# Half the gather buffers, early gate weights in the freed megabyte, and one down matrix asked for sooner

## What is computed

```python
for e in range(N_EXPERTS):                       # 32 experts, 3 matrices of 1 MB each
    act = jax.nn.silu(hf @ w_gate[e]) * (hf @ w_up[e])
    y = y + combine[:, e:e + 1] * (act @ w_down[e])
```

## Time and profile before

| what | value |
|---|---|
| median of 3 executions | 1311.11 us |
| the profiled execution, its own time | 1308.09 us |
| its span on the core | 1306.3 us |
| PE busy | 1217.3 us, 93% of the span |
| DVE busy | 558.0 us, 43% |
| ACT busy | 307.9 us, 24% |
| POOL busy | 245.1 us, 19% |
| moved by DMA | 213.06 MB, mean 163 GB/s |
| granted TensorE clock, mean | 0.978 |

### The profile page before, as it was taken

How to read it: one execution, slowest core, us unless ns; L and a number is a source line. 1 busy time by engine, 2 the same in 40 slices (tenths; PEclk the granted TensorE clock), 3 DMA queues, 4 the chain that set the end, 5 groups by cost and what they waited for, 6 DMA issues and landing times.

```text
span 1306.3 us, 13442 instructions
## 1 busy us (share of the span) xinstructions
PE 1217.3 (93%) x5000; PEld 686.0 (53%) x5000; DVE 558.0 (43%) x1424; ACT 307.9 (24%) x725; POOL 245.1 (19%) x214
## 2 busy tenths in 40 slices
PE   6999989999989999999999899999999879977884
PEld 3555434455544444588884446776664544433342
DVE  2214493566547751208972367422232623222221
ACT  4313643433310000224022245300011311111110
POOL 6000023354500000071600030312300021211100
PEclk9999999999989999999999999999999979998898
DMA  9625112224265612313131102202257589999994
GB/s 330 115 73 129 65 70 60 104 76 144 86 207 191 225 57 89 113 65 129 65 119 74 57 9 65 70 1 65 65 191 323 213 314 385 407 403 406 416 404 143
DMA packets 92248, 213.06 MB, mean 163 GB/s; under 512 B 20186, under 2 KB 51306, under 8 KB 79848
## 3 DMA queue, kind: packets, MB, share of 16 engines
q1 hardware_dynamic: 78800, 191.56, 39.8%
q0 software_dynamic: 10176, 17.96, 5.7%
q10 hardware_dynamic: 3200, 2.61, 0.6%
HBM read 205.73 MB, written 14.75 MB: 169 GB/s over the span
## 4 chain that ended last, share of the span: by engine, by line
PE 76%; DVE 7%; SPq 6%; DMA 5%; ACT 3%; issue 2%; ACTq 0%; POOL 0%; POOLq 0%; DVEq 0%
PE PS L2280 7%; PE PS L995 6%; PE PS L638 5%; SPq L2766 5%; PE PS L1488 4%; PE PS L1410 4%; PE PS L2343 4%; PE PS L1671 4%; PE PS L1673 4%; PE PS L2449 3%; PE PS L2897 3%; PE PS L1419 2%; DMA AN<-in_w_down 2%; DMA X<-in_w_up 2%; PE PS L1717 2%; PE PS L1729 2%
## 5 line engine op out<-in xcount | busy, mean ns | idle before, releaser
L995 PE MATMUL PS<-HT,W 128*128 128x512 f32 x256 | 123.5, 605 | 1.8 <-ACT AN L1159 1.7
L1257 POOL TENSOR_SCALAR AN<-AN,SM 128x128 f32<-128x128 f32 (+3 forms) x64 | 72.1, 1134 | 197.1 <-DVE SM L1349 197.1
L1280 DVE SCALAR_TENSOR_TENSOR AN<-AN,COLA 128x256 f32<-128x256 f32 x168 | 85.3, 508 | 5.0
L2897 PE MATMUL PS<-AN,HT 128*64 128x512 f32 x192 | 62.4, 636 | 11.8 <-DMA X<-in_w_up 8.1
L638 PE MATMUL PS<-W,HT 128*128 128x512 f32 (+1 forms) x192 | 70.4, 528 | 0.0
L2976 DVE TENSOR_TENSOR HT<-HT,PS 128x256 f32<-128x256 f32 x16 | 6.7, 421 | 141.8 <-ACT HT L2954 141.8
L995 PEld LDWEIGHTS PS<-HT,W 128*128 128x128 f32 x256 | 44.1, 192 | 38.6 <-issue 35.0
L1488 PE MATMUL PS<-W,AN 128*128 128x512 f32 x128 | 57.2, 608 | 1.9 <-DVE GBC L1294 1.9
L1410 PE MATMUL PS<-HT,W 128*128 128x512 f32 x128 | 58.1, 599 | 0.0
L2449 PE MATMUL PS<-W,AN 128*128 128x512 f32 x128 | 57.6, 597 | 0.0
L1239 ACT ACTIVATE AN<-PS,SM 128x128 f32<-128x128 f32 (+3 forms) x64 | 33.7, 526 | 93.8 <-DVE SM L1328 93.5
(11 more groups left out here) (511 smaller groups left out, 2266.8 us busy)
## 6 DMA issues: line engine op xcount, KB each, us to landing
W<-in_w_in SPq DMA_DIRECT2D x14, 2048.0 KB, 8.9
W<-in_w_down SPq DMA_DIRECT2D x20, 1024.0 KB, 25.3
AN<-in_w_ada SPq DMA_DIRECT2D x17, 1024.0 KB, 5.2
AN<-in_w_gate SPq DMA_DIRECT2D x17, 1024.0 KB, 25.1
AN<-in_w_up SPq DMA_DIRECT2D x17, 1024.0 KB, 25.3
AN<-in_w_down SPq DMA_DIRECT2D x12, 1024.0 KB, 25.3
W<-in_w_gate SPq DMA_DIRECT2D x10, 1024.0 KB, 24.8
W<-in_w_up SPq DMA_DIRECT2D x10, 1024.0 KB, 28.1
```

Of the source, the lines that this page charges most:

```text
L995: t = pe.matmul(u.ap, w[:, c, tile(m)], hT[:, c, :], start=c == 0, stop=c == 7)
L1257: pool.tensor_scalar(PU[u % 5][:, 0:n], PU[u % 5][:, 0:n], RSUM[:, u:u + 1], None, ALU.mult).then_inc(*sc_pool.up(u))
L1280: dve.scalar_tensor_tensor(out=a, in0=wt[:, c, :], scalar=ca["c2"][:, c:c + 1], in1=a, op0=ALU.mult, op1=ALU.add).then_inc(*ada_dve.up(p, c))
L2897: t = pe.matmul(u.ap[r, :].rearrange("p (n f) -> p n f", n=2), XGT[e % 2][:, c, r], w_gu(3 * e + half)[:, c], start=c == 0, stop=c == 7)
```

## The change

There are two gather buffers instead of four. The upper half of `XN` becomes `W3`, 1 MB, which holds one gate matrix: that of the first expert of the fourth pair, until now half a of group 9. SP asks for it right after the first gather has landed, ahead of the second residual write, and no longer at `first_pe`. Both halves of group 8 are asked for together, where only half a was until now. POOL's order becomes: gathers 0 and 1, then gather 2, scatter 0, gather 3, scatter 1 and so on, so gather `e + 1` follows scatter `e - 2`. Tile 3 is done in the order of tile 0, all gates first, and reads its first gate from `W3`.

```diff
-    XG = [XN[:, i, :] for i in range(4)]
+    XG = [XN[:, i, :] for i in range(2)]
+    W3 = XN[:, 2:4].rearrange("p i (c f) -> p (i c) f", c=4)
...
-    xg_in = sig(*[f"xg{i}_in" for i in range(4)], step=16)
+    xg_in = sig(*[f"xg{i}_in" for i in range(2)], step=16)
+    fourth_in = sig("fourth_gate_in", step=16)
...
             for m in (3 * e, 3 * e + 1):
-                if m - NE in (0, 1) and n == 0:
+                if m == NE and n == 0:
+                    continue
+                if m == NE + 1 and n == 0:
                     ws.wait_ge(*first_pe.at())
...
-        sp_expert(sp, ws, 8, (0,))
+        sp_expert(sp, ws, 8)
         ws.wait_ge(*xg_in[0].at(0))
+        ws.wait_ge(*xn_out.at())
+        sp.dma_start(W3, wg_[NE // 3].rearrange("(p c) f -> p c f", c=8)).then_inc(*fourth_in.up())
         sp_residual(sp, ws, 1)
-        sp_expert(sp, ws, 8, (1,))
         sp_expert(sp, ws, 7, (1,))
...
-        wg.wait_ge(*(B.use("xg", e - 4, 1).full if e > 3 else B.use("xT3", 3, 1).full))
+        wg.wait_ge(*(B.use("xg", e - 2, 1).full if e > 1 else B.use("xT3", 3, 1).full))
...
-        for e in range(e0, e0 + 3):
-            pool_gather(pool, wg, e)
+        pool_gather(pool, wg, e0)
+        pool_gather(pool, wg, e0 + 1)
         for e in range(e0, e1 + 1):
-            if e + 3 < e1:
-                pool_gather(pool, wg, e + 3)
+            if e0 < e and e + 1 < e1:
+                pool_gather(pool, wg, e + 1)
             if e > e0:
                 pool_scatter(pool, wg, e - 1)
...
-        if e in (0, NP - 2, NP - 1):
+        if e in (0, NE // 3, NP - 2, NP - 1):
             for n in range(2):
-                if e:
+                if e >= NP - 2:
                     wp.wait_ge(*last_in[e - NP][n].at())
                 else:
-                    wp.wait_ge(*exp_in[0].at(0))
-                    wp.wait_ge(*exp_in[1].at(1))
+                    wp.wait_ge(*exp_in[0].at(3 * e))
+                    wp.wait_ge(*exp_in[1].at(3 * e + 1))
+                if e == NE // 3:
+                    wp.wait_ge(*fourth_in.at())
                 for c in range(8):
                     for half in range(2):
                         r = slice(64 * half, 64 * half + 64)
-                        t = pe.matmul(u.ap[r, 256 * n:256 * n + 256], XGT[e % 2][:, c, r], w_gu(3 * e + half)[:, c, n],
+                        t = pe.matmul(u.ap[r, 256 * n:256 * n + 256], XGT[e % 2][:, c, r],
+                                      W3[:, c] if (e, n, half) == (NE // 3, 0, 0) else w_gu(3 * e + half)[:, c, n],
                                       start=c == 0, stop=c == 7)
```

More of the change, by code:

```diff
@@ L2828, in pool_gather @@
         wg.wait_ge(*xn_out.at())
-        wg.wait_ge(*(B.use("xg", e - 4, 1).full if e > 3 else B.use("xT3", 3, 1).full))
+        wg.wait_ge(*(B.use("xg", e - 2, 1).full if e > 1 else B.use("xT3", 3, 1).full))
         pool.indirect_dma_start(
-            out=XG[e % 4], out_offset=None, in_=xnd, in_offset=bass.IndirectOffsetOnAxis(ap=TID[:, e:e + 1], axis=0),
-            bounds_check=S - 1, oob_is_err=False).then_inc(*xg_in[e % 4].up(e))
+            out=XG[e % 2], out_offset=None, in_=xnd, in_offset=bass.IndirectOffsetOnAxis(ap=TID[:, e:e + 1], axis=0),
+            bounds_check=S - 1, oob_is_err=False).then_inc(*xg_in[e % 2].up(e))
     def pool_scatter(pool, wg, e):
@@ L2858, in pe_turn_in @@
             wp.wait_ge(*u.free)
-            wp.wait_ge(*xg_in[e % 4].at(e))
+            wp.wait_ge(*xg_in[e % 2].at(e))
             for c4 in range(4):
-                t = pe.transpose(u.ap[:, tile(c4)], fv(XG[e % 4][:, 4 * q + c4:4 * q + c4 + 1], [[8, 128]]), ident)
+                t = pe.transpose(u.ap[:, tile(c4)], fv(XG[e % 2][:, 4 * q + c4:4 * q + c4 + 1], [[8, 128]]), ident)
             t.then_inc(*u.filled)
```

## The result

The changed kernel takes **1316.63 us** (median of 20, from 1311.76 to 1318.75), the kernel before 1311.6 us (median of 20, from 1307.98 to 1313.67). The ratio is 1.0037 with a 95% interval of [1.0028, 1.0047], so it is slower by 3.7 to 6.2 us. That lies above the range that was given, 1306.6 to 1314.4 us, and on the other side of the forecast of 0.6 us faster.

What follows compares the result with a forecast made beforehand. Reading expert weights bounds the kernel, so only earlier DMA idle time counts. Gain 2.6, less 0.3, less 0.9: 1.4 us faster; by bytes 0.5 slower; taken as 0.6 faster, median 1310.5 us, range 1306.6 to 1314.4 us.

Steps and rivals of the forecast that it cites:

- What bounds the kernel: Expert stage: bound by reading its weights; only earlier DMA idle time counts, 5.8 us between 1046 and 1053.6 us.
- I cost this at nothing; were it delayed by the whole 2.6 us, the first gather would be late by 0.7 us: Scratch copy's last write, landing at 1047.2 us: early half b costs it nothing, with 1.9 us of cover before the first gather.
- It lands near 1060, and half b of group 7 follows then: Second residual write, behind early gate and one gather: 2.6 + 2.6 + about 1.2 us, landing near 1060 us.
- The queue runs dry just ahead of 1073.5, for 0.9 us: From 1053.6 to 1073.5 us: 19.0 us of DMA work for 19.9 us to fill, a new gap of 0.9 us.
- The rival of more gaps: Dry queue near 1060, ahead of 1066.6 and of 1073.5 us: 0.8 us slower, up to 2 us at each; chance 0.18.
- The gain of 2.6 us for half b: Idle stretch from 1046 to 1048.6 us: filled by half b of group 8, 2.6 us faster if nothing else happens.
- Two gathers at 1.6 us, offset by the stock: Gathers of tiles 3 and 4, moved into busy DMA time: 1.6 us, against 3.0 us of stock left at 1073.5 us.
- Both megabytes count: Rival: early gate and half b both fall into idle time before the bound stretch, 5.2 us faster, 1305.9 us; chance 0.09.
- Gathers later, tile 3 in halves: Gather 3 is there by 1087.7 us, wanted at 1091.81; tile 3's 64 matmuls take 7.3 us; both cost nothing.
- The last 15.4 us untouched: From the landing of the last weights at 1290.95 us to the span's end: about 15.4 us, touched by neither edit.
- The range: Median of the changed kernel: 1306.6 to 1314.4 us, from half b in full to more gaps, with 2 us scatter.
- The fixed cost of 2.0 us: Restarted DMA queue: about 2.0 us per transfer; if all idle at the one gap, the sum would be 1 us worse.

Runs made afterwards that it cites:

- half b put back: The changed kernel with half b of group 8 back in its old slot behind the residual write: 1314.34 us, ratio 1.0027 to the kernel before.
- half b after the copy: Half b of group 8 asked for once the scratch copy has landed: in the changed kernel 1313.07 us, ratio 1.0015; in the kernel before 1312.68 us, 0.9999.
- residual first: The changed kernel with the second residual write issued ahead of the early gate: 1315.79 us, ratio 1.0043 to the kernel before.
- early gate placed well: The changed kernel with residual write, early gate and half b of group 8 in this order behind the first gather: 1312.75 us, ratio 1.0014.
- two buffers alone: The kernel before with two gather buffers and the changed order of POOL, without the early gate: 1313.86 us, ratio 1.0023.

## Why the prediction was wrong, point by point

- **What bounds the kernel**: right. The bound stretch runs at 405 GB/s after (402 before), and only what happens before it counts. The idle stretch was where it was said to be, and half b filled it.
- **"I cost this at nothing; were it delayed by the whole 2.6 us, the first gather would be late by 0.7 us"**: this step failed. The write was delayed by 3.1 us, and the cover was not the 1.9 us up to the gather's start but 1.0 us, since the gather's instruction needs some 0.9 us between its release and its start (the write landed at 1054.84, the gather started at 1055.74; before, VectorE's table was done at 1048.25 and the gather started at 1049.12). The first gather, and all of tile 0 with it, was 2.1 us late. The delay is shown by half b put back, its price by half b after the copy: 2.9 us with two buffers, 2.6 us with four, each known to 2 us or so.
- **"It lands near 1060, and half b of group 7 follows then"**: mis-sized. Behind the early gate the residual write took 10.8 us and not 7.4. SP stood for 10.0 us, and with it not only group 7's half b but the next gate, whose release had come some 2 us before. That I had written of one transfer held up and not of the queue behind it is the second fault. What it cost in time is not shown: residual first shortened the write to 5.0 us and was no faster, and early gate placed well, with 5.1 us, took as long as half b after the copy with two buffers, with 10.7 us (those two differ in half b's place too).
- **"The queue runs dry just ahead of 1073.5, for 0.9 us"**: the mechanism was right and the place wrong. I summed the stock up to the ups at 1066 as if it could all be asked for at once. It is dry at each point where the next request waits for PE, and the first of them is the gates that tile 0 releases, 24 us behind R. The hole there is 3 us in the changed kernel, where the late tile and the held queue add to it. The rival of more gaps came nearest, with a first gap near 1060 (22 us behind R) and 0.8 to 2 us slower; the loss was more than twice that, and it had neither the collision nor the low clock. The place at 1073.5 shows too, as a share of 0.54 and 0.47, once the earlier ones are filled.
- **The gain of 2.6 us for half b**: failed. With nothing in its way it was worth 0.1 us, give or take 1.8 us: 0.9999 [0.9986, 1.0013].
- **Two gathers at 1.6 us, offset by the stock**: two buffers alone cost 3.0 us. Their last landing is 1.6 to 2.7 us later than in the profile of the kernel before whose tile 0 was as late as theirs; in one of two profiles the low clock adds 1.7 us. The exact split stays open.
- **Both megabytes count**: wrong. The Trainium skill's advice to issue a DMA early and wait late (DMA: Bandwidth & Descriptors, rules for kernel authors) helps at most in one of two cases here: the gate added to what could be asked for, and moved the last landing to 252.6 us (254.8 and 256.0 with two buffers alone), though the times can't tell the two apart; half b did not add to it.
- **Gathers later, tile 3 in halves**: right, both cost nothing. PE waits for no gather behind tile 0, and tile 3's 64 matmuls took 6.91 us where 32 take 6.87.
- **The last 15.4 us untouched**: wrong by 2.0 us, by PE's clock in the last matmuls. No row of before hinted at it.
- **The range**: its upper end does not follow from the words. More gaps, 1311.9 to 1313.1 us, with 2 us more gives up to 1315.1 and not 1314.4; 1306.6 and 1314.4 are the forecast less and plus 0.3%. The result lies above either. That the change was a small one was foreseen, its direction was not.

The fixed cost of 2.0 us that the prediction takes from the Trainium skill (DMA: Bandwidth & Descriptors, anatomy of one DMA) is given there for transfers that GpSimd issues, and those at the gaps are SP's. The sum did not use it.

The same page of the Trainium skill states (queues, rings and completion order) that each DMA engine takes turns between the queues that have work. The trace shows that this does not keep a short write short: 512 KB asked for on ScalarE's queue took 3.9 us beside the reads that were then queued, and 7.0 us with one more megabyte on SP's queue, and landed 0.4 us behind that megabyte.

## What to carry to other kernels

When a stage is bound by a stream, list the times at which each transfer may first be asked for, and sum the stock from each of these times to the next; asking sooner helps only if it enlarges the stock at the first point where it runs out. Before filling an idle stretch of the DMA engines, look for the small transfer in it that someone waits for, and put the bulk behind its landing, not ahead of it. A write that gates the next request in a queue should be tried at its front, but look at what the queue can ask for next: here the wait shrank from 10.8 to 5.0 us and the time did not.

## What was not expected of the hardware

- The 1 MB residual write took 4.0 us where it was asked for ahead of the gathers (9.2 us behind R), 4.9 to 6.5 us where it was asked for behind the first of them, and 10.2 to 10.8 us when 1 MB of reads was asked for 0.4 us ahead of it on the same queue (three kernels): 5 us more for 2.6 us of reads.
- The gap of the first gather's release to its start, 0.9 us in both kernels, ate half of the 1.9 us that looked like slack in a view of start times.
- The last 16 matmuls took 3.67 us in four of four profiles of the one kernel and 5.37 us in four of four of the other, with no difference in PE's work ahead of them that these views show. Of the ten other profiles six have 5.1 to 5.4 us and four 3.7 us.
